# One expert load of 128 rows, issued as one piece of 64 rows and eight pieces of eight

## The reference

```python
def _moe(x, router_w, router_b, w1, b1, w2, b2):
    logits = x.astype(jnp.float32) @ router_w.astype(jnp.float32) + router_b.astype(jnp.float32)
    top_logits, top_idx = lax.top_k(logits, TOP_K)                      # 4 of 32
    gates = jax.nn.softmax(top_logits, axis=-1)
    ...
    for e in range(N_EXPERTS):
        a = x @ w1[e] + b1[e]                                           # 1024 x 2048, float32
        glu = jnp.minimum(a[:, ::2], SWIGLU_LIMIT)
        lin = jnp.clip(a[:, 1::2], -SWIGLU_LIMIT, SWIGLU_LIMIT)
        act = glu * jax.nn.sigmoid(SWIGLU_ALPHA * glu) * (lin + 1)
        out = out + combine[:, e:e + 1] * (act @ w2[e] + b2[e])         # 1024 x 1024, float32
```

## Time and profile before

| what | before |
|---|---|
| median of three runs | 1108.04 us |
| the profiled execution: its own time, its span | 1109.17 us, 1107.4 us |
| TensorE matmul busy | 1052.6 us, 95% |
| VectorE, ScalarE, GpSimd busy | 260.5, 172.9, 30.9 us |
| granted TensorE clock, mean | 0.994 |
| bytes moved by the DMA engines | 431.94 MB, 390 GB/s over the span |
| SyncE's load queue | 428.52 MB, 93.1% of the sixteen engines' time |

### The profile page before, as it was taken

How to read it: one execution, slowest core, us unless ns; L and a number is a source line. 1 busy time by engine, 2 the same in 40 slices (tenths; PEclk the granted TensorE clock), 3 DMA queues, 4 the chain that set the end, 5 groups by cost and what they waited for, 6 DMA issues and landing times.

```text
span 1107.4 us, 12108 instructions
## 1 busy us (share of the span) xinstructions
PE 1052.6 (95%) x5229; PEld 469.6 (42%) x5229; DVE 260.5 (24%) x523; ACT 172.9 (16%) x417; POOL 30.9 (3%) x67
## 2 busy tenths in 40 slices
PE   8999999999999999999999899898998899899986
PEld 6767856343433434343433334242434343433322
DVE  4745544112121202020202011121212020202013
ACT  3562023010101111010101102020201010101102
POOL 6000022000000000000000000000000000000000
PEclk9999999999999999999999899999999999999999
DMA  9942896999999999999999999999999999999994
GB/s 304 358 175 76 298 365 234 396 410 429 426 428 427 429 426 428 428 428 427 428 427 426 429 428 427 428 427 428 428 427 428 428 427 426 428 428 426 428 420 165
DMA packets 52265, 431.94 MB, mean 390 GB/s; under 512 B 5350, under 2 KB 16302, under 8 KB 26768
## 3 DMA queue, kind: packets, MB, share of 16 engines
q1 hardware_dynamic: 50144, 428.52, 93.1%
q0 software_dynamic: 608, 2.04, 0.6%
q10 hardware_dynamic: 1456, 0.57, 0.2%
HBM read 427.63 MB, written 3.48 MB: 389 GB/s over the span
## 4 chain that ended last, share of the span: by engine, by line
PE 64%; DMA 34%; issue 1%; DVE 1%; ACT 1%; ACTq 0%; SPq 0%; DVEq 0%
DMA ring<-in_expert_w 33%; PE ps L2034 29%; PE ps L2090 9%; PE ps L1617 5%; PE ps L1956 3%; PE ps L1930 3%; PE ps L1598 3%; PE ps L1761 2%; PE ps L1633 2%; PE ps L1703 1%; PE ps L1769 1%; PE ps L1940 1%; PE ps L1860 1%; PE ps L2009 1%; PE ps L2062 0%
## 5 line engine op out<-in xcount | busy, mean ns | idle before, releaser
L2034 PE MATMUL ps<-ring,mem 128*64 128x512 f32 x2040 | 461.2, 599 | 21.6 <-DMA ring<-in_expert_w 21.6
L2034 PEld LDWEIGHTS ps<-ring,mem 128*64 128x64 f32 x2040 | 146.3, 137 | 302.9 <-issue 300.5
L2090 PE MATMUL ps<-ring,mem 128*64 128x512 f32 x1024 | 223.9, 594 | 4.4 <-ACT mem L921 3.7
L1411 DVE TENSOR_TENSOR mem<-mem,ps 128x1024 f32<-128x1024 f32 x30 | 36.6, 1222 | 455.3 <-PE ps L1956 421.1
L2090 PEld LDWEIGHTS ps<-ring,mem 128*64 128x64 f32 x1024 | 72.5, 137 | 144.0 <-issue 136.4
L926 ACT ACTIVATE mem<-ps 128x264 f32<-128x264 f32 x16 | 6.3, 391 | 443.1 <-PE ps L2009 443.0
L1930 PEld LDWEIGHTS ps<-mem 128*128 128x128 f32 x600 | 65.4, 173 | 13.4 <-issue 12.2
L1930 PE MATMUL ps<-mem 128*128 128x128 f32 x600 | 70.1, 276 | 0.0
L1617 PE MATMUL ps<-ring 128*128 128x266 f32 x256 | 60.3, 391 | 0.0
L1956 PE MATMUL ps<-mem 128*128 128x512 f32 x120 | 60.0, 620 | 0.0
L1617 PEld LDWEIGHTS ps<-ring 128*128 128x128 f32 x256 | 47.6, 190 | 11.0 <-issue 3.1
(11 more groups left out here) (306 smaller groups left out, 576.5 us busy)
## 6 DMA issues: line engine op xcount, KB each, us to landing
ring<-in_expert_w SPq DMA_DIRECT2D x180, 2048.0 KB, 39.7
ring<-in_expert_w SPq DMA_DIRECT2D x17, 1024.0 KB, 28.1
ring<-in_w_in SPq DMA_DIRECT2D x6, 2048.0 KB, 21.7
ring<-in_expert_w SPq DMA_DIRECT2D x12, 512.0 KB, 10.2
ring<-in_w_in SPq DMA_DIRECT2D x2, 1024.0 KB, 8.7
ring<-in_state_rec SPq DMA_DIRECT2D x4, 512.0 KB, 10.5
ring<-in_w_out SPq DMA_DIRECT2D x1, 2048.0 KB, 14.6
ring<-in_w_out SPq DMA_DIRECT2D x2, 1024.0 KB, 6.3
```

Source lines behind the costliest of these rows:

```text
L1411: dve.tensor_tensor(h3[:, m], h3[:, m], ps[:, 4 + 2 * m:6 + 2 * m, :].rearrange("p a n -> p (a n)"), ALU.add)\
L2034: done = mm(ps[CAP * e:CAP * e + CAP, b, :], xgT3[:, t, CAP * e:CAP * e + CAP], w_late[:, col - 2 * D:col - 2 * D + HALF] if first and (t, ...
L2090: done = mm(ps[CAP * e:CAP * e + CAP, 4 + half, :], actT3[:, 4 * v + t, CAP * e:CAP * e + CAP], ring[:, slot[e], col:col + HALF], start=(v ...
```

## The change

Load g = 12 x 12 + 6, the seventh w1 load of pair twelve (unit 3, expert 24), is no longer one DMA of 128 rows. It goes out as one DMA for partitions 0 to 63 and eight DMAs for eight partitions each, from 64 on. All nine write the same bytes to the same place as before and add to the same semaphore, and `PIECES` says nine for this load. In a DMA of eight rows, eight of the sixteen DMA engines carry one row each.

```diff
-        PIECES = {2: 2, 9: 2, SLOTS: 4, SLOTS + 1: 4, SLOTS + 3: 2}
+        SHIFTED, ROWS = 12 * LOADS + 6, 8
+        PIECES = {2: 2, 9: 2, SLOTS: 4, SLOTS + 1: 4, SLOTS + 3: 2, SHIFTED: 1 + P // (2 * ROWS)}
...
+            def load_shifted(g):
+
+                p, j = g // LOADS, g % LOADS
+                to, part = cut(ring[:, place_of(g), :], 2 * D), w1_v[2 * p + j % 2, j // 2]
+                for rows in [slice(0, P // 2)] + [slice(at, at + ROWS) for at in range(P // 2, P, ROWS)]:
+                    sp.dma_start(to[rows], part[rows]).then_inc(ring_in[place_of(g)], 16)
...
                 for g in range(SLOTS + 4, in_pieces):
                     sp.wait_ge(w_used, g - SLOTS + 1)
-                    load(g)
+                    if g == SHIFTED:
+                        load_shifted(g)
+                    else:
+                        load(g)
```

## The result

The changed kernel takes 1123.43 us (median of four runs, 1120.71 to 1127.07) against 1108.11 of the kernel before on the same chip: ratio 1.0136, 95% interval 1.0117 to 1.0154, so 15.3 us slower (13.0 to 17.1). The forecast was 1118.0, with 1105 to 1125 as its range of eight in ten. The profiled execution took 1124.0 us with a span of 1122.3 us, 14.9 us over the span before. Lines of the kernel above the change keep their work; numbers from 400 on are 1 to 11 higher: L2034 is now L2045, L2009 is L2020, L2090 is L2101, L1972 is L1983, and the nine pieces are issued at L484.

What follows compares the result with a forecast made beforehand. The DMA engines, full with weight loads, were taken as the bound; crowding would land the load after 4.90 + 9.80 = 14.70 us instead of 4.90, so 1108.04 + 9.8 = 1117.8, say 1118 us; eight-in-ten range 1105 to 1125.

Steps and rivals of the forecast that it cites:

- the forecast's own case: At the changed load: crowding at half rate, 1112 to 1123 us with 1118 as its centre; chance 0.47.
- case 3: At the small pieces: four engines in step on four neighbouring partitions, an eighth of the rate; 1124 to 1128 us; chance 0.12.
- The bound: From pair twelve to the end: DMA engines stay full at 428 GB/s, so time lost there is found again at the end.
- Issues cost nothing: On SyncE at pair twelve: eight more issues of 0.40 us, 3.2 us, fit into a pause of up to 12.1 us.
- Crowding at half rate: At the changed load: writing half the partitions runs at 214 GB/s, landing after 14.70 us instead of 4.90, plus 9.8 us.
- The evidence for half the rate: From 23 to 26 us: bias loads to 32 partitions each, engines full but moving 240 GB/s, against 428 in the stream.
- The byte shift: At the changed load: eight engines carry 12 rows, eight carry 4, where all had 8; plus or minus 2.45 us.
- rival 1: At the changed load: the eight engines given more rows are ahead, no crowding, so 2.45 us faster, 1105.6; chance 0.17.
- The assumption on the other eight engines: Behind the big piece: the other eight engines, already at the next load, write their 64 rows into the upper partitions too.
- Rivals 1 and 2: Byte shift without crowding: first, eight engines ahead, 1105.6, chance 0.17; second, level or behind, 1110.5, chance 0.14.
- 4 (nothing): At the changed load: a partial lead or partial crowding cancels the shift, or pieces use all sixteen engines; 1108; chance 0.10.
- What would show it: Signs: GB/s below 400 at about 880 to 905 us; expert-load waits and TensorE's ring total each up about 10 us.

Runs made afterwards that it cites:

- nine pieces by columns: Against the kernel before, the load cut into nine pieces over all 128 partitions, one of 8 KB per row and eight of 1 KB: 1108.72 us, ratio 1.0004.
- the halves: Against the kernel before, the load cut into partitions 0 to 63 and 64 to 127: 1119.97 us, 1.0108; at pair two 1117.31 us, 1.0085.
- the mirrored change: Against the kernel before, one piece for partitions 64 to 127 and eight pieces of eight neighbours in 0 to 63: 1122.84 us, ratio 1.0136.
- strided pieces: Against the kernel before, eight-row pieces taking every fourth partition of a 32-partition block: upper half 1123.06 us, 1.0124; lower half 1117.43 us, 1.0082.

## Why the prediction was right, and where a term was too small

The measured 1123.43 lies inside the range that was given, 1105 to 1125, but 0.4 us above the forecast's own case, 1112 to 1123; it is the room left for case 3, whose mechanism is not what the runs show, that holds it. The direction and the mechanism were foreseen, the size by about two thirds.

**The bound** was read rightly: nothing of the loss was given back, at pair twelve or at pair two. After 930 us the stream runs at 428 GB/s as before, and the output stage is later by 14.40 us.

**Issues cost nothing**: right, although one took 1.13 us in place of 0.40. The nine pieces by columns show that neither they nor the nine completions cost anything.

**Crowding at half rate** was the right mechanism, in the right window, at nearly the right rate (184 to 233 against 214 GB/s). Its length was too small, and this is the step that was mis-sized: "The load is landed 4.90 + 9.80 = 14.70 us after it began". Those 14.70 us at half rate lose 7.35 us of the stream. The windows lose 12.3 us, over some 25 us. What is shown is that the halves alone lose 9.6 us where the same sum gives 4.9. The forecast took all engines to pass the changed load together, with only its own rows slowed. The traces show that they are not together, by the last windows of the kernel before, and that the load *before* the changed one lands 4.57 us late. Both fit that engines at the changed load slow those that are not there yet. How much of the factor of two comes from that drift is not settled; at pair two it is 7.9 / 4.9 = 1.6 rather than 2.0. Nor is it known why the change at pair two ran below half the rate in two windows (154 and 177 GB/s).

**The evidence for half the rate** was thinner than the forecast made it: the stretch at 23 us moved 0.72 MB in 192 packets, 3.8 KB each, where a packet of the stream has 14.6 KB (25.61 MB in 1756 packets from 540 to 600 us). Small packets were a rival for its 240 GB/s. The two halves, with the full 16 KB rows, gave 223 to 233 GB/s and settled it.

**The byte shift**, 2.45 us: the rest beyond the loss is 2.6 us for the change. Over the six kernels with pieces of eight rows this rest averages (2.6 + 2.1 + 0.8 + 0.6 + 0.3 + 1.7) / 6 = 1.4 us, over the seven without such pieces (0.2 - 1.3 + 0.0 + 0.8 - 1.0 - 0.4 + 0.1) / 7 = -0.2. So something of about 1.6 us comes with these pieces, and single spans are too rough to say more. Together, 7.35 + 2.45 = 9.8 forecast stands against 12.3 + 2.6 = 14.9 measured on the span.

That the rest comes near 2.45 is luck in part, since the reason given for it, eight engines level or behind, is not what the end of the run shows. In windows of 0.8 us the share stays between 0.44 and 0.59 for 2.4 to 4.8 us in the kernel before and in all seven kernels without pieces of eight rows, and for 0.8 us at most in all six kernels with them. The eight engines that took the extra rows would have been ahead by 5 to 6 us at the end, as rival 1 had it, and a gain should have followed. None did: after the change one or two engines land last, some 4 us behind the others (shares of 0.13 and 0.08). Why these are late stays open.

**The assumption on the other eight engines**, that the upper rows are what they carry, doesn't show with pieces of neighbours, where the mirrored change costs the same. It does show with strided pieces, 14.3 us in the upper half against 8.7 in the lower, and in the direction that it says.

**The rivals.** Rivals 1 and 2 (byte shift without crowding) and 4 (nothing) are out by the windows, though the lead of eight engines on which rival 1 rests is there. Rival 3 was near in size (1124) but not in kind: it wanted engines in step at an eighth of the rate for 19.6 us, and neither the windows nor the strided pieces show that.

**What would show it.** GB/s below 400 at a share of 1.0 between 880 and 905 us: right. Two waits behind 885 us and no more: right, 12.6 us in place of about 10. TensorE's total wait for the ring up by the same sum: wrong, since the second wait is filed under "issue" and later ones shrink. Such shrinking was named as a sign that the eight engines were ahead; the halves, which shift nothing between engines, show it too. The sum of waits by name is no measure of a delay; the start of the last stage is.

What stays open is how an engine is chosen for a row of a piece with fewer than 128 partitions, as no row here names an engine, and whether the partitions or the places in HBM are what crowds. The runs show which cuts are free (two or four pieces that take every second or every fourth partition of all 128, and nine by columns) and which are not.

## What to carry to other kernels

If a load must go out in several DMAs while the DMA engines are the bound, cut it by columns or by interleaved partitions (every second, every fourth), never by ranges of partitions: the same two or four pieces cost 0 us one way and 10 to 11 us the other, for 2 MB of 430. Pieces of eight rows were slow in every placement tried (8.7 to 15.3 us). Read GB/s beside the DMA share; the share stays at 1.0 while half of the rate is gone. A hole in a saturated stream cost its full length at both places tried, also where the engine that it feeds didn't notice it. To see whether the DMA engines are level, look at the last windows in which they work: a step at half of the share is half of the engines done before the rest.

## What the hardware showed beyond that

- Neighbouring quarters of the partitions are filled at the rate of neighbouring halves: 229 and 228 against 229 and 233 GB/s.
- One crowded load of 2 MB holds the whole stream at half rate for about 20 us (halves) to 25 us (the change), four to five times the 4.90 us that a load takes.
- The sixteen engines are not level: at the end of the kernel before one set of eight is 5 to 6 us ahead of the other, and one load that gives the leading set more rows makes them nearly level (read from the share; no view names an engine).
- An issue of a piece took 10.14 / 9 = 1.13 us on SyncE, where two whole loads were issued in 0.80 us.
- In these windows TensorE's granted clock fell below full speed only behind its own idle stretches (2.78 and 1.01 us busy of 5, then 0.73 and 0.59 granted; 0.00 busy from 900 to 905 us, then 0.50). 0.50 is the lower of its two levels, 1.2 of 2.4 GHz, for the whole window; the others are both levels in one window.
